# Seven half-depth products in place of eight for three pairs of feed-forward blocks

## The chip, the cores and the metric

The kernel runs on one core of a Trainium2 chip. The metric is the device time in microseconds (us) of one execution. Five engines of the core work here: TensorE (PE, matrix products), VectorE (DVE), ScalarE (ACT), GpSimd (POOL) and SyncE (SP), whose queue issues most of the DMAs. Each engine works through its own list in order and waits on semaphores that the others raise.

## The reference

Two decoder layers work on 256 tokens of width 1024. Each has a mixer (two kinds of attention, not touched here) and a feed-forward part, to which the change belongs:

```
h = _rmsnorm(x, g_pre_ffn) * (1.0 + sc2) + sh2
f = (jax.nn.silu(h @ w_gate) * (h @ w_up)) @ w_down
return x + gt2 * _rmsnorm(f, g_post_ffn)
```

The hidden width is 2816. Everything is float32. The vectors sc2, sh2 and gt2 come from a product of silu(c) with `w_ada`, which the kernel accumulates in 512 KB pieces beside the other work.

## The kernel before

**Tiles.** The 256 tokens are two tiles of 128 (t = 0, 1). The activations lie transposed, in eight slices k of 128 rows of depth. A float32 product is made of three fast ones (`product`, L1481 to L1485): high part by high part, high by low of the weights, low by high. The hidden width is cut into 11 blocks j of 256 columns. A block is projected upwards by `up(l, j, t)`: 128 tokens by 512 columns (256 of the gate, 256 of the other branch) over eight slices, so 24 products of 128x512 for each t. Then ScalarE takes the silu, VectorE multiplies the halves (`ffn_m`, L1460, called a gate below), TensorE transposes the result (`turn_m`), ScalarE and VectorE split it into high and low parts, and `down_chunk(l, j, t)` projects it downwards with 12 products of 128x512.

**Weights.** All weights come in units of 128x2048 elements (1 MB). An upward projection of a block uses two units (slices 0 to 3, and 4 to 7), a downward one uses one. A unit is loaded into one of three `raw` buffers (SP, L468), ScalarE copies its high part to `w_hi` (L654) and VectorE subtracts for its low part `w_lo` (L1006). `w_hi` and `w_lo` are rings of five: the split of a unit waits until TensorE has used the unit five places earlier. The load of a unit waits for the split of the unit that lay in its buffer.

**Order.** All orders are written out by hand. For block j TensorE runs `up(j, 0)`, `up(j, 1)`, `down_chunk(j-1, 0)`, `turn_m(j, 0)`, `turn_m(j, 1)`, `down_chunk(j-1, 1)`. VectorE runs the split of one unit, the two gates, a split, a piece of the modulation vector (L1034), the two low parts of `ffn_m` (L1208) and a split. In layer 1 eight such pieces lie in blocks 0 to 7, one a block. After the eighth, GpSimd sums the vector over the partitions (PARTITION_ALL_REDUCE, L555).

## Time and profile before

| what | us |
|---|---|
| median of 3 runs | 846.04 |
| lowest and highest run | 845.91, 846.12 |
| the profiled execution | 845.91 |
| its span, first to last instruction | 844.1 |

The span is what the views below cover. The rest of an execution's time lies around it. TensorE is busy for 99% of the span, VectorE for 77%, ScalarE for 53%. Layer 1's feed-forward part runs from about 651 us to 838 us of the span. What is busy on TensorE is modelled: a product of 128x512 has a duration of 0.39 us in the rows, while the next one starts 0.23 us after it. In a row of a timeline the first number is the start, the second the duration, and in brackets stands how long the engine was idle before it and what ended that.

### The profile page before, as it was taken

The numbers are of one execution on the slowest core, as the hardware profiler recorded it, in microseconds if no ns is written. First come the engines' busy times: TensorE is split into PE (matmuls) and PEld (weight loads), VectorE is DVE, ScalarE is ACT, GpSimd is POOL, SyncE is SP. The second block draws the span as 40 slices with busy tenths as digits, with TensorE's granted clock in tenths as the row PEclk, the third lists the DMA queues.
The fourth block names the chain that finished last, engine by engine and source line by source line (L and its number), as shares of the span: only waits on it lengthen the run. The fifth ranks groups of instructions, "written<-read, shape, count | busy, mean of one in ns | idle before, by whom it ended". The sixth has DMA issues, their size and how long they took to land.

```text
span 844.1 us, 11561 instructions
## 1 busy us (share of the span) xinstructions
PE 835.2 (99%) x4155; PEld 694.2 (82%) x4155; DVE 646.4 (77%) x1150; ACT 446.3 (53%) x723; POOL 122.2 (14%) x92
## 2 busy tenths in 40 slices
PE   8999999999999999999999999999999999999997
PEld 6877888888888888888888788888888888888885
DVE  5798889888788776786689899898787866545743
ACT  5665555565757434433476556565565745334422
POOL 5500300301210021030420040040040000000300
PEclk9999999999999999999999999999999999999999
DMA  8996676576417788787438756766642576664611
GB/s 342 415 360 233 217 257 252 203 270 224 144 57 299 290 282 324 251 305 278 183 120 310 284 204 219 276 214 243 221 150 100 198 276 213 247 236 177 223 51 51
DMA packets 34795, 194.10 MB, mean 230 GB/s; under 512 B 4273, under 2 KB 4529, under 8 KB 17714
## 3 DMA queue, kind: packets, MB, share of 16 engines
q1 hardware_dynamic: 33410, 189.64, 61.4%
q0 software_dynamic: 1328, 3.71, 1.3%
q8 instruction: 34, 0.56, 0.3%
q14 instruction: 23, 0.19, 0.1%
HBM read 192.29 MB, written 1.05 MB: 229 GB/s over the span
## 4 chain that ended last, share of the span: by engine, by line
PE 95%; DMA 3%; DVE 1%; SPq 0%; issue 0%; DVEq 0%; ACT 0%
PE ps L1483 26%; PE ps L1485 26%; PE ps L1484 26%; PE ps L1596 4%; DMA wide_t<-scale_first 3%; PE ps L1660 2%; PE ps L1520 1%; PE ps L1521 1%; PE ps L1527 1%; PE ps L1681 1%; PE ps L1682 1%; PE ps L1659 1%; PE ps L1680 1%; PE ps L1642 1%; PE ps L1612 1%; PE ps L1834 0%
## 5 line engine op out<-in xcount | busy, mean ns | idle before, releaser
L1006 DVE TENSOR_TENSOR w_lo<-raw,w_hi 128x2048 fp32r<-128x2048 f32 (+2 forms) x128 | 294.8, 2309 | 60.2 <-ACT w_hi L654 59.1
L1483 PE MATMUL ps<-w_hi,t_hi 128*128 128x512 f32 (+2 forms) x776 | 306.9, 395 | 1.0 <-DVE w_lo L1006 0.9
L1485 PE MATMUL ps<-w_hi,t_lo 128*128 128x512 f32 (+2 forms) x776 | 300.0, 387 | 0.0
L1484 PE MATMUL ps<-w_lo,t_hi 128*128 128x512 f32 (+2 forms) x776 | 299.4, 386 | 0.0
L654 ACT ACTIVATE w_hi<-raw 128x2048 fp32r<-128x2048 f32 (+2 forms) x130 | 244.8, 1885 | 25.5 <-DMA raw<-w_stream 16.9
L1483 PEld LDWEIGHTS ps<-w_hi,t_hi 128*128 128x128 f32 x776 | 145.8, 188 | 32.1 <-DVE w_lo L1006 1.9
L1485 PEld LDWEIGHTS ps<-w_hi,t_lo 128*128 128x128 f32 x776 | 145.7, 188 | 30.2
L1484 PEld LDWEIGHTS ps<-w_lo,t_hi 128*128 128x128 f32 x776 | 146.0, 188 | 27.6
L555 POOL PARTITION_ALL_REDUCE wide_t<-wide_t x20 | 80.0, 3998 | 555.7 <-DVE wide_t L1034 554.8
L1034 DVE SCALAR_TENSOR_TENSOR wide_t<-ada,cs,wide_t 128x1024 f32<-128x1024 f32 x80 | 110.3, 1379 | 1.0 <-DMA ada<-w_ada 0.7
L966 ACT ACTIVATE relu<-ps 128x256 f32<-128x256 f32 x44 | 17.0, 386 | 147.4 <-PE ps L1485 147.4
L1483 PE MATMUL ps<-w_hi,m_hi 128*128 128x512 f32 x208 | 84.3, 405 | 0.0
L1485 PE MATMUL ps<-w_hi,m_lo 128*128 128x512 f32 x208 | 81.4, 391 | 0.0
L1484 PE MATMUL ps<-w_lo,m_hi 128*128 128x512 f32 x208 | 81.0, 389 | 0.0
L1460 DVE TENSOR_TENSOR ffn_m<-relu,ps 128x256 f32<-128x256 f32 x44 | 18.2, 418 | 75.0 <-ACT relu L966 74.9
L727 ACT ACTIVATE qkT<-ps 128x512 f32<-128x512 f32 x24 | 14.4, 599 | 71.9 <-PE ps L1596 45.4
L1485 PEld LDWEIGHTS ps<-w_hi,m_lo 128*128 128x128 f32 x208 | 39.0, 188 | 8.6
L1484 PEld LDWEIGHTS ps<-w_lo,m_hi 128*128 128x128 f32 x208 | 39.2, 188 | 7.3
L1483 PEld LDWEIGHTS ps<-w_hi,m_hi 128*128 128x128 f32 x208 | 39.1, 188 | 7.1
L681 ACT ACTIVATE pj<-ps 128x384 f32<-128x384 f32 x32 | 15.7, 492 | 38.5 <-PE ps L1485 38.5
L747 ACT ACTIVATE m_hi<-ps 128x256 fp32r<-128x256 f32 (+1 forms) x48 | 17.3, 400 | 18.2 <-PE ps L1596 18.2
L545 POOL MEMSET wide_t<- 128x1024 f32 x10 | 9.6, 961 | 90.8 <-DVE x L1319 74.4
(226 smaller groups left out, 911.4 us busy)
## 6 DMA issues: line engine op xcount, KB each, us to landing
raw<-w_stream SPq DMA_DIRECT2D x126, 1024.0 KB, 5.2
ada<-w_ada SPq DMA_DIRECT2D x80, 512.0 KB, 5.6
wide_t<-gains POOLq DMA_DIRECT2D x7, 512.0 KB, 4.6
raw<-w_stream SPq DMA_DIRECT2D x4, 656.0 KB, 7.4
mixed<-scale_first SPq DMA_DIRECT2D x2, 1024.0 KB, 9.7
wide_t<-shift_first SPq DMA_DIRECT2D x4, 512.0 KB, 10.5
wide_t<-scale_first SPq DMA_DIRECT2D x2, 1024.0 KB, 12.7
ada<-shift_first SPq DMA_DIRECT2D x4, 512.0 KB, 12.5
```

Of the source, the lines that this page charges most:

```text
L555: nc.gpsimd.partition_all_reduce(acc[:, cols], tables[i][:, cols], P, bass.bass_isa.ReduceOp.add).then_inc(s_reduced, 1)
L654: nc.scalar.activation(w_hi[:, U % RING, a:n], src[:, a:n], ACT.Copy).then_inc(s_hi, 1)
L747: nc.scalar.activation(dst, src, ACT.Copy).then_inc(s_act_hi, 1)
L966: nc.scalar.activation(ffn_s[:, t, :], ps[:, QKT + t, 0:256], ACT.Silu).then_inc(s_silu, 1)
L1006: nc.vector.tensor_tensor(w_lo[:, U % RING, a:n], src[:, a:n], w_hi[:, U % RING, a:n].bitcast(F32), ALU.subtract).then_inc(s_lo, 1)
L1034: nc.vector.scalar_tensor_tensor(out=buf[:, :], in0=src, scalar=cs[:, k:k + 1], in1=buf[:, :], op0=ALU.mult, op1=ALU.add).then_inc(s_adaus ...
L1460: nc.vector.tensor_tensor(ffn_m[:, t, :], ffn_s[:, t, :], ps[:, QKT + t, 256:512], ALU.mult).then_inc(s_m, 1)
L1483: nc.tensor.matmul(dst, hi, w_h, start=first, stop=False)
L1484: nc.tensor.matmul(dst, hi, w_l, start=False, stop=False)
L1485: return nc.tensor.matmul(dst, lo, w_h, start=False, stop=last)
L1596: ins = nc.tensor.transpose(dst[:, i * P:(i + 1) * P], blk, ident)
L1660: nc.tensor.matmul(ps[:, SCO, P:3 * P], q[:, P:SEQ], k, start=True, stop=True).then_inc(s_sco, 1)
```

## The change

In layer 1, blocks (3, 4), (6, 7) and (8, 9) are projected upwards in pairs (`TWINS`). The two token tiles, the two halves of the depth and the two blocks make a product of two-by-two matrices of tiles. Such a product is made with seven tile products in place of eight, at the price of sums of tiles before it and after it. Each tile product is 12 products of 128x512 (`seventh`, over four slices). Layer 0 is as before.

- **Sums of the tokens** are made once (`add_tokens`, at block 1): five VectorE instructions, one over 128x2048 elements, four over 128x512. ScalarE splits off the high part of the result, and at block 2 VectorE the low part (`sums_low`).
- **Sums of the weights** (`add_weights`): the seven products use seven weight units in place of four. Four of the seven are sums, which VectorE makes with four additions over 128x2048 for each pair, in the memory of `mixed` and of `raw`. All seven are split into high and low parts.
- **Sums of the products** (`add_products`): five VectorE additions over 128x512 for each pair, and one copy by ScalarE. Product 5 continues in the accumulator of product 1, and product 6 in that of product 4, once those have been read: TensorE waits for the second and the third of the additions there.
- **Loads**: each weight is still loaded once. One unit of each pair goes to `mixed`. The other three stay in the three `raw` buffers until products 4 and 5 have been split.
- **The pieces** of the modulation vector move: blocks 0, 1, 2 and 5 of layer 1 take 1, 2, 2 and 3 of them.

```diff
+TWINS = ((), (3, 6, 8))
+TWIN_SUMS = (1, 4, 3, 6)
...
-    return (1, 1, 1, 1, 1, 1, 1, 1, 0, 0, 0), (9,)
+    return (1, 2, 2, 0, 0, 3, 0, 0, 0, 0, 0), (8,)
...
+            def twin_hi(l, j):
+                p = twin_no(l, j)
+                ahead, behind = up_splits(l, j)
+                split_hi(l, ahead[0])
+                wait_twin(act, l, j, 0)
+                nc.scalar.activation(twin_a, ps[:, QKT, :], ACT.Copy).then_inc(s_kept, 1)
+                for u in behind[:4]:
+                    split_hi(l, u)
+                act.wait_ge(s_twin, 5 * p + 4)
+                silu(l, j, 0, twin_c[:, 0:256], -1.0)
+                silu(l, j, 1, twin_b[:, 0:256], -1.0)
+                split_hi(l, behind[4])
+                silu(l, j + 1, 0, ps[:, QKT, 0:256])
+                act.wait_ge(s_twin, 5 * p + 5)
+                silu(l, j + 1, 1, twin_a[:, 0:256])
+                split_hi(l, behind[5])
+                m_hi_split(l, j, 0)
+                m_hi_split(l, j, 1)
+                split_hi(l, behind[6])
+                split_hi(l, behind[7])
+                m_hi_split(l, j + 1, 0)
+                m_hi_split(l, j + 1, 1)
...
+            def add_weights(U, e):
+                start = U - e
+                upper, lower, corner = (stored(*SOURCE[start + i]) for i in (4, 5, 2))
+                dve.wait_ge(s_lo, U + 1)
+                if e == 0:
+                    dve.wait_ge(upper[1], upper[2])
+                    nc.vector.tensor_tensor(w_sum, w_sum, upper[0], ALU.add).then_inc(s_w_sum, 1)
+                    dve.wait_ge(lower[1], lower[2])
+                    nc.vector.tensor_tensor(upper[0], upper[0], lower[0], ALU.add).then_inc(s_w_sum, 1)
+                else:
+                    nc.vector.tensor_tensor(w_sum, w_sum, (lower if e == 1 else corner)[0], ALU.add).then_inc(s_w_sum, 1)
...
+            def twin_lo(l, j):
+                ahead, behind = up_splits(l, j)
+                up = slice(256, 512)
+                split_lo(l, ahead[0])
+                split_lo(l, behind[0])
+                split_lo(l, behind[1])
+                add_products(l, j, twin_a, twin_a, SCO, 3, 1)
+                add_products(l, j, twin_b, twin_a, PTB, 1, 2)
+                split_lo(l, behind[2])
+                add_products(l, j, twin_b, twin_b, OUT, 4, 3)
+                split_lo(l, behind[3])
+                add_products(l, j, twin_c, twin_a, PTB, 5, 4)
+                gate_m(l, j, 0, twin_c[:, up], -1.0)
+                gate_m(l, j, 1, twin_b[:, up], -1.0)
+                add_products(l, j, twin_a, twin_a, OUT, 6, 5)
+                split_lo(l, behind[4])
+                m_lo_split(l, j, 0)
+                m_lo_split(l, j, 1)
+                gate_m(l, j + 1, 0, ps[:, QKT, up])
+                gate_m(l, j + 1, 1, twin_a[:, up])
+                split_lo(l, behind[5])
+                if j in ffn_pieces(l)[1]:
+                    make_table(4 * l + 3 + ffn_pieces(l)[1].index(j))
+                split_lo(l, behind[6])
+                split_lo(l, behind[7])
+                m_lo_split(l, j + 1, 0)
+                m_lo_split(l, j + 1, 1)
...
+                    if j == sums_step(l):
+                        add_tokens(l)
+                    elif j == sums_step(l) + 1:
+                        sums_low(l)
...
+            def twin_up(l, j):
+                p = twin_no(l, j)
+                before = 2 * (l * N_FF + j - 1)
...
+                pe.wait_ge(s_m, before + 1)
+                seventh(0, QKT, t_hi, t_lo, 0, 0)
+                pe.wait_ge(s_sums_lo, sums_no(l))
+                pe.wait_ge(s_act_lo, l * N_SPLIT + turn_no("m", 2 * (j - 1)))
+                seventh(1, PTB, sums_hi, sums_lo, 1, 1)
+                pe.wait_ge(s_kept, p + 1)
+                seventh(2, QKT, t_hi, t_lo, 1, 0, first=False)
+                pe.wait_ge(s_m, before + 2)
+                seventh(3, SCO, sums_hi, sums_lo, 0, 0)
+                pe.wait_ge(s_act_lo, l * N_SPLIT + turn_no("m", 2 * (j - 1) + 1))
+                seventh(4, OUT, sums_hi, sums_lo, 0, 1)
+                pe.wait_ge(s_twin, 5 * p + 2)
+                seventh(5, PTB, sums_hi, sums_lo, 1, 0, first=False)
+                pe.wait_ge(s_twin, 5 * p + 3)
+                seventh(6, OUT, t_hi, t_lo, 1, 1, first=False)
+                down_chunk(l, j - 1, 0)
+                turn_m(l, j, 0)
+                pe.wait_ge(s_twin, 5 * p + 5)
+                turn_m(l, j, 1)
+                down_chunk(l, j - 1, 1)
+                down_chunk(l, j, 0)
+                turn_m(l, j + 1, 0)
+                turn_m(l, j + 1, 1)
+                down_chunk(l, j, 1)
```

Two places of VectorE's list show how the work moves. The first is layer 1's blocks 0 to 2, in the kernel before. Here `w_lo<-raw,w_hi` is the split of a weight unit, `ffn_m<-relu,ps` a gate, `m_lo<-ps,m_hi` the low part of a gated block, and `wide_t<-ada,cs,wide_t` a piece.

```order
L1006 TENSOR_TENSOR w_lo<-raw,w_hi 128x2048
L1208 TENSOR_TENSOR m_lo<-ps,m_hi 128x2x128
L1460 TENSOR_TENSOR ffn_m<-relu,ps 128x256 x2
L1006 TENSOR_TENSOR w_lo<-raw,w_hi 128x2048
L1034 SCALAR_TENSOR_TENSOR wide_t<-ada,cs,wide_t 128x1024
L1208 TENSOR_TENSOR m_lo<-ps,m_hi 128x2x128 x2
L1006 TENSOR_TENSOR w_lo<-raw,w_hi 128x2048 x2
L1460 TENSOR_TENSOR ffn_m<-relu,ps 128x256 x2
```

The same place in the changed kernel, from the same split to the gates of block 1:

```order
L1156 TENSOR_TENSOR w_lo<-raw,w_hi 128x2048
L1179 TENSOR_TENSOR token_sums<-t_hi,t_lo 128x2048
L1180 TENSOR_TENSOR token_sums<-token_sums 128x4x128
L1181 TENSOR_TENSOR token_sums<-token_sums 128x4x128
L1182 SCALAR_TENSOR_TENSOR token_sums<-token_sums 128x4x128
L1184 SCALAR_TENSOR_TENSOR token_sums<-token_sums 128x4x128
L1442 TENSOR_TENSOR m_lo<-ps,m_hi 128x2x128
L1212 TENSOR_TENSOR ffn_m<-relu,ps 128x256 x2
```

And on from there, to the gates of block 2:

```order
L1156 TENSOR_TENSOR w_lo<-raw,w_hi 128x2048
L1268 SCALAR_TENSOR_TENSOR wide_t<-ada,cs,wide_t 128x1024
L1442 TENSOR_TENSOR m_lo<-ps,m_hi 128x2x128 x2
L1156 TENSOR_TENSOR w_lo<-mixed,w_hi 128x2048
L1168 TENSOR_TENSOR mixed<-mixed,raw 128x2048
L1170 TENSOR_TENSOR raw<-raw 128x2048
L1268 SCALAR_TENSOR_TENSOR wide_t<-ada,cs,wide_t 128x1024
L1190 TENSOR_TENSOR token_sums_lo<-token_sums,token_sums_hi 128x2048
L1156 TENSOR_TENSOR w_lo<-mixed,w_hi 128x2048
L1172 TENSOR_TENSOR mixed<-mixed,raw 128x2048
L1212 TENSOR_TENSOR ffn_m<-relu,ps 128x256 x2
```

Five token sums now stand ahead of the gates of block 1. Between those gates and the gates of block 2 stand three additions of weights, one more piece, and the low part of the token sums.

The second place is where pair (6, 7) meets pair (8, 9), from the last sum of products of the first to the low parts of block 7. Before, the two blocks' share here was the repeating pattern of a gate pair, three splits, a piece and two low parts.

```order
L1156 TENSOR_TENSOR w_lo<-mixed,w_hi 128x2048
L1168 TENSOR_TENSOR mixed<-mixed,raw 128x2048
L1170 TENSOR_TENSOR raw<-raw 128x2048
L1442 TENSOR_TENSOR m_lo<-ps,m_hi 128x2x128 x2
L1212 TENSOR_TENSOR ffn_m<-relu,ps 128x256
L1212 TENSOR_TENSOR ffn_m<-relu,pj 128x256
L1156 TENSOR_TENSOR w_lo<-mixed,w_hi 128x2048
L1172 TENSOR_TENSOR mixed<-mixed,raw 128x2048
L1156 TENSOR_TENSOR w_lo<-raw,w_hi 128x2048
L1156 TENSOR_TENSOR w_lo<-mixed,w_hi 128x2048
L1172 TENSOR_TENSOR mixed<-mixed,raw 128x2048
L1442 TENSOR_TENSOR m_lo<-ps,m_hi 128x2x128 x2
```

Two additions stand ahead of block 6's low parts, and two more among the splits ahead of block 7's.

## Rows read from the trace of the kernel before

**Rows 1.** The page: busy time, and TensorE and its granted clock in 40 slices.
```profile
PE 835.2 (99%) x4155; PEld 694.2 (82%) x4155; DVE 646.4 (77%) x1150; ACT 446.3 (53%) x723; POOL 122.2 (14%) x92
...
PE   8999999999999999999999999999999999999997
...
PEclk9999999999999999999999999999999999999999
```

**Rows 2.** A stretch: length, busy PE, PEld, DVE, ACT, POOL, granted clock, DMA share, GB/s.
```profile
655.00:831.00 176.00, 176.00 (x801) 145.16 (x801) 104.38 (x96) 77.82 (x85) 9.09 (x5) 1.00 0.53 194
```

**Rows 3.** Timeline of TensorE: start, duration, line, operation.
```profile
678.35 0.60 PE L1596 MATMUL ps<-const,ffn_m 128*128 128x128 f32 x4
...
698.34 0.39 PE L1483 MATMUL ps<-w_hi,t_hi 128*128 128x512 f32 x1
...
709.22 0.39 PE L1483 MATMUL ps<-w_hi,m_hi 128*128 128x512 f32 x1
```

**Rows 4.** Groups by line and shape: busy us, mean ns, idle before and releaser.
```profile
L1006 DVE TENSOR_TENSOR w_lo<-raw,w_hi 128x2048 fp32r<-128x2048 f32 x31 | 74.0, 2407 | 16.5 <-ACT w_hi L654 16.5
...
L1034 DVE SCALAR_TENSOR_TENSOR wide_t<-ada,cs,wide_t 128x1024 f32<-128x1024 f32 x8 | 10.2, 1280 | 0.0
...
L1460 DVE TENSOR_TENSOR ffn_m<-relu,ps 128x256 f32<-128x256 f32 x22 | 9.1, 419 | 51.7 <-ACT relu L966 51.7
...
L1242 DVE SCALAR_TENSOR_TENSOR pj<-pj,rstd,wide_t 128x512 f32<-128x512 f32 x4 | 2.8, 750 | 0.1
...
L1273 DVE TENSOR_TENSOR pj<-ps,wide_t 128x512 f32<-128x512 f32 x4 | 2.7, 680 | 0.0
...
L1280 DVE TENSOR_TENSOR pj<-x,wide_t 128x448 f32<-128x448 f32 x2 | 1.2, 615 | 0.0
...
L1280 DVE TENSOR_TENSOR pj<-x,wide_t 128x96 f32<-128x96 f32 x4 | 1.0, 245 | 0.0
```

**Rows 5.** Timeline of VectorE in blocks 0, 1, 2, 3 and 4.
```profile
674.25 2.29 DVE L1006 TENSOR_TENSOR w_lo<-raw,w_hi 128x2048 fp32r<-128x2048 f32 x1 [0.56 <-ACT w_hi L654]
676.46 0.42 DVE L1208 TENSOR_TENSOR m_lo<-ps,m_hi 128x256 fp32r<-128x256 f32 x1
676.79 0.74 DVE L1460 TENSOR_TENSOR ffn_m<-relu,ps 128x256 f32<-128x256 f32 x2
...
694.83 2.29 DVE L1006 TENSOR_TENSOR w_lo<-raw,w_hi 128x2048 fp32r<-128x2048 f32 x1 [1.38 <-ACT w_hi L654]
...
704.40 0.42 DVE L1460 TENSOR_TENSOR ffn_m<-relu,ps 128x256 f32<-128x256 f32 x1 [1.01 <-ACT relu L966]
...
721.19 0.42 DVE L1460 TENSOR_TENSOR ffn_m<-relu,ps 128x256 f32<-128x256 f32 x1 [0.99 <-ACT relu L966]
```

**Rows 6.** Timeline of ScalarE: splits of high parts in blocks 0, 1 and 3.
```profile
662.77 3.71 ACT L654 ACTIVATE w_hi<-raw 128x2048 fp32r<-128x2048 f32 x2
...
672.28 1.93 ACT L654 ACTIVATE w_hi<-raw 128x2048 fp32r<-128x2048 f32 x1 [2.12 <-DMA raw<-w_stream]
...
698.60 1.92 ACT L654 ACTIVATE w_hi<-raw 128x2048 fp32r<-128x2048 f32 x1 [0.53 <-PE ps L1485]
```

**Rows 7.** Timeline of GpSimd and VectorE around the eighth piece's sum.
```profile
782.43 7.48 POOL L555 PARTITION_ALL_REDUCE wide_t<-wide_t  x2 [125.99 <-DVE wide_t L1034]
782.91 8.15 DVE L1006 TENSOR_TENSOR w_lo<-raw,w_hi 128x2048 fp32r<-128x2048 f32 x2
```

**Rows 8.** The tile raw: landing of its loads, then one issue on SyncE's timeline.
```profile
DMA to landing us min/median/max: 4.6/5.5/7.3
...
697.15 0.33 SPq L468 DMA_DIRECT2D raw<-w_stream  x1
```

**Rows 9.** The end: the last matmul, then half-microsecond stretches (granted clock third from the end).
```profile
837.99 0.39 PE L1485 MATMUL ps<-w_hi,m_lo 128*128 128x512 f32 x1
...
842.00:842.50 0.50, 0.00 (x0) 0.00 (x0) 0.00 (x0) 0.00 (x0) 0.00 (x0) 1.00 1.05 410
842.50:843.00 0.50, 0.00 (x0) 0.00 (x0) 0.00 (x0) 0.00 (x0) 0.00 (x0) 0.64 0.98 377
```

More of the change, by code:

```diff
@@ L347, in hybrid_decoder_trunk, with stored @@
         shift_at = (wide_t[:, 0, :], wide_t[:, 1, :], ada[:, 0, :], ada[:, 1, :])
[L349 to L363 removed]
+        def stored(kind, n):
+            if kind == "spare":
+                return scale_at[n], s_spare[n], 16
+            if kind == "sum":
+                return w_sum, s_sum_in, 16 * (n + 1)
+            return raw[:, n % RAW, :], s_raw[n % RAW], 16 * (n // RAW + 1)
+        def raw_at(U):
+            return stored(*SOURCE[U])
         cs_wide = qkT[:, 0:KT * 32].rearrange("p (k n) -> p k n", k=KT)
@@ L949, in _ @@
                 border(l, True)
-                for j in range(N_FF):
-                    ahead, behind = up_splits(j)
+                for j, *both in ffn_steps(l):
+                    if both:
+                        twin_hi(l, j)
+                        continue
+                    ahead, behind = up_splits(l, j)
                     for u in ahead[:1]:
@@ new lines, in add_tokens @@
+            def add_tokens(l):
+                upper, lower = slice(0, 4), slice(4, KT)
+                one, two = slice(0, P), slice(P, 2 * P)
+                dve.wait_ge(s_act_lo, l * N_SPLIT + turn_no("h2", 3))
+                link(nc.vector.tensor_tensor(sums[:, :, :], t_hi[:, :, :].bitcast(F32), t_lo[:, :, :].bitcast(F32), ALU.add))
+                link(nc.vector.tensor_tensor(sums[:, lower, two], sums[:, lower, two], sums[:, upper, two], ALU.subtract))
+                link(nc.vector.tensor_tensor(sums[:, upper, two], sums[:, upper, one], sums[:, upper, two], ALU.subtract))
+                link(nc.vector.scalar_tensor_tensor(out=sums[:, upper, one], in0=sums[:, lower, two], scalar=-1.0,
+                                                    in1=sums[:, upper, one], op0=ALU.mult, op1=ALU.subtract))
+                nc.vector.scalar_tensor_tensor(out=sums[:, lower, one], in0=sums[:, lower, one], scalar=-1.0,
+                                               in1=sums[:, upper, one], op0=ALU.mult, op1=ALU.subtract).then_inc(s_sums, 1)
@@ new lines, in sums_low, with add_products @@
+            def sums_low(l):
+                dve.wait_ge(s_sums_hi, sums_no(l))
+                nc.vector.tensor_tensor(sums_lo[:, :, :], sums[:, :, :], sums_hi[:, :, :].bitcast(F32),
+                                        ALU.subtract).then_inc(s_sums_lo, 1)
+            def add_products(l, j, to, of, bank, after, count):
+                p = twin_no(l, j)
+                wait_twin(dve, l, j, after)
+                if count == 1:
+                    dve.wait_ge(s_kept, p + 1)
+                else:
+                    dve.wait_ge(s_twin, 5 * p + count - 1)
+                nc.vector.tensor_tensor(to, of, ps[:, bank, :], ALU.add).then_inc(s_twin, 1)
@@ L1441, in _ @@
                 border(l, True)
-                for j in range(N_FF):
-                    ahead, behind = up_splits(j)
+                for j, *both in ffn_steps(l):
+                    if both:
+                        twin_lo(l, j)
+                        continue
+                    ahead, behind = up_splits(l, j)
                     many = ffn_pieces(l)[0][j]
+                    if j == sums_step(l):
+                        add_tokens(l)
+                    elif j == sums_step(l) + 1:
+                        sums_low(l)
                     for u in ahead[:1]:
@@ L1887, in up, with seventh @@
                 ins.then_inc(s_up, 1)
+            def twin_up(l, j):
+                p = twin_no(l, j)
+                before = 2 * (l * N_FF + j - 1)
+                def seventh(e, bank, hi, lo, half, t, first=True):
+                    U = BASE[l] + twin_unit(l, j) + e
+                    pe.wait_ge(s_lo, U + 1)
+                    for i in range(4):
+                        k, tokens, cols = 4 * half + i, slice(t * P, (t + 1) * P), slice(512 * i, 512 * i + 512)
+                        parts = ((hi, w_hi), (hi, w_lo), (lo, w_hi))
+                        for n, (h, w) in enumerate(parts):
+                            ins = nc.tensor.matmul(ps[:, bank, :], h[:, k, tokens], w[:, U % RING, cols],
+                                                   start=first and i + n == 0, stop=i + n == 5,
+                                                   skip_group_check=not first)
+                    ins.then_inc(s_used, 1)
+                pe.wait_ge(s_m, before + 1)
[22 more added lines that the diff above has]
+                down_chunk(l, j, 1)
             def turn_m(l, j, t):
@@ L1966, in _ @@
                 turn_m(l, 0, 0)
-                for j in range(1, N_FF):
+                for j, *both in ffn_steps(l)[1:]:
+                    if both:
+                        twin_up(l, j)
+                        continue
                     up(l, j, 0)
```

205 lines of the change are left out of this document (145 added, 60 removed).

## The prediction

> **What bounds the kernel now.** I read the page first, then the stretches of layer 1's feed-forward part, then the groups by shape and the timelines of the engines. The page shows TensorE busy for 99% and in every slice of 40, at the full granted clock [rows 1]. From 655 to 831 us it is busy for all 176 us, while VectorE has 104.4 us of work and ScalarE 77.8 [rows 2]. So TensorE's list is the time here, and a product less is time less, as long as the others keep up. The reader should also see how little slack VectorE has in the end: it waits 51.7 us for silus in front of its gates and 16.5 us in front of its splits [rows 4], and the change fills that.
>
> TensorE's pace: `up(3, 0)` and `up(3, 1)`, 48 products, take from 698.34 to 709.22 us [rows 3], so 0.2267 us each. A block lasts 721.19 - 704.40 = 16.79 us [rows 5]: 72 products are 16.32, and the two transposes of a block 0.47.
>
> **What is removed.** Each pair loses one tile product of 12 products: 3 x 12 x 0.2267 = 8.2 us of TensorE. A pair falls from 33.6 to 30.9 us.
>
> **What VectorE gets.** A split takes 2.21 us from start to next start (674.25 to 676.46) and is known to the others 2.32 us after its start (694.83, issue at 697.15) [rows 5, 8]. Gates and low parts follow at 0.33 (0.42 for one, 0.74 for two) [rows 5]. A piece is 1.28 long, 1.20 to the next [rows 4].
>
> The additions of weights are not in the trace. The nearest rows are float32 sums with two SBUF inputs: 245 ns for 96 elements and 615 for 448 [rows 4], so 1.051 ns an element, and for 2048 elements 245 + 1952 x 1.051 = 2297 ns: the length of a split. I take the split's 2.21 from start to start, 2.30 as the upper bound, and 1.1 (twice the rate) as the lower, since no row has this shape in plain float32. The Trainium skill ("VectorE: DVE Perf Modes", section "Why `tensor_tensor` can't do 2×_2P or 4×") says that float32 instructions with one tensor input can run at twice the rate, and those with two cannot. By that rule the additions cost what the splits cost, and the bound of 1.1 falls away. The rows above bear it out for the small sums only.
>
> A sum of products reads PSUM and SBUF at 128x512: 0.68 long, 0.61 to the next [rows 4]. The token sums: 2.29, then two at 0.69 and two at 0.75 [rows 4], each waiting for the one before, for which I add 0.07 four times: 5.45. Their low part is a split, 2.21.
>
> New work in all: three more units a pair, 9 x 2.21 = 19.9; 12 additions, 26.5; 15 sums of products, 9.2; token sums 7.7. That is 63.2 us on top of 104.4, so 167.6 us. TensorE would need 176 - 8.2 = 167.8. VectorE has no slack left, and it works in order among handoffs, so TensorE will wait. For a pair followed by a pair VectorE has nine splits, four additions, five sums, four gates and four low parts: 19.9 + 8.8 + 3.1 + 2.6 = 34.4 us against 30.9.
>
> **Where TensorE waits.** I follow both lists from the same point, 676.46 us, with ScalarE's splits at 1.80 apart (3.71 for two less 1.91) and ready about 1.95 after their start (672.28, and VectorE at 674.25), and TensorE's results known 0.26 after a unit (698.34 to 698.60) [rows 3, 5, 6].
>
> *Block 1.* The token sums stand ahead of the gates: 676.46 + 5.45 + 0.33 (low part of block 0) + 0.33 (gate) + 0.11 = 682.68. The transposes of block 1 stand at 678.35 [rows 3]. Wait: 4.3.
>
> *Block 2.* ScalarE makes the high part of the token sums from 682.0 to 683.8 and only then splits a weight unit, which VectorE has at 685.77. Then it runs seven of the size of a split (three splits, three additions, the low part of the token sums) 15.5, two pieces 2.4, two low parts 0.7, a gate 0.3, and two waits on itself 0.2: 704.85, known at 704.96. TensorE leaves its last wait at 682.68, with 0.57 for the transposes (0.1 of it a second wait) and 72 products, 16.32, ahead of it: 699.57. Wait: 5.4.
>
> *Pair (3, 4).* Product 5 needs the second sum of products. From block 2's first gate VectorE has 0.3, a split 2.2, a piece 1.2, two low parts 0.7, a split 2.2, an addition 2.3, a piece 1.2, three splits 6.6 and two sums 1.3, a handoff 0.1: 723.05. TensorE again has 0.57 and 72 products: 721.85. Wait: 1.2. The next unit's load waits until the sum in `raw` is split, at 717.3; with a landing in 4.7 us, near the least of 4.6 [rows 8], ScalarE starts at 722.0, and product 6 waits 1.1. With the median of 5.5 this becomes 1.9.
>
> *Pair (6, 7).* The eighth piece now ends in block 5, so GpSimd's sum falls on the pair. Beside it two splits took 8.15 us [rows 7] in place of 2.21 + 2.29: some 3.6 more, before in a place with slack. From product 6 of pair (3, 4), at 726.88, TensorE runs 108 products and four transposes to the end of `up(5, 1)`, 752.30; a handoff, a silu (0.28) and a high part later VectorE can split, at 754.79: five splits 11.1, two pieces 2.4, two low parts 0.7, an addition 2.3, the delay 3.6, two sums 1.3, a handoff 0.1: 776.27. TensorE has 84 more products and two transposes after 752.30 (19.04 + 0.47): 771.82. Wait: 4.5.
>
> *From pair to pair.* Product 5's unit is split at 772.7; only then is the next unit loaded (4.7), made high (1.95) and low (2.21); then come a sum 0.7, two silus 0.6 and the high part of the next pair's first unit: 784.82. Block 6's low parts stand behind ScalarE's split of product 1 of the next pair, which needs VectorE's addition: 784.82 + 2.2 + 0.1 + 2.2 + 0.1 (VectorE), + 1.8 + 0.4 (ScalarE), + 0.4 = 792.13, against 787.72. Wait: 4.4. Product 1 of pair (8, 9) needs the accumulator that block 7's low part frees, and that stands behind three splits and two additions: 793.01 + 5 x 2.21 + 0.2 + 0.4 = 804.72, against 800.76. Wait: 4.0. After that VectorE has only splits, and nothing waits.
>
> Small waits beside these come to 0.3. Sum: 4.3 + 5.4 + 1.2 + 1.1 + 4.5 + 4.4 + 4.0 + 0.3 = 25.2 us of waits, less 8.2 of products: 17.0 longer. The same lists, followed for the kernel before, end TensorE at 838.1; the trace has 837.99 + 0.39 [rows 9]. The tail behind it stays. The profiled execution's 845.91 becomes 862.9; it lies 0.1 below the median, so 863.
>
> **Bounds.** With landings at 5.5 the waits are 26.8 (+18.6, 864.5). With handoffs shorter by 0.06 each it is +15.8 (861.7). With additions at 2.30 it is at most 12 x 0.09 = 1.1 more (864). With additions at 1.1, 3.3 goes from block 2, 1.2 from pair (3, 4), 1.1 from each of the next two, 2.2 from the last: +8.1, 854.
>
> **Rivals.**
> *The clock falls in the waits.* After the last matmul's end at 838.38 the granted clock holds until about 842.6 and then halves [rows 9]: 4.2 us of idleness did it. Four of my waits are longer (4.3, 5.4, 4.5, 4.4), one is 4.0. Against it: these are at the edge. The return of the clock is not in the trace; with 5 us at half speed each fall costs 2.5. But the loss after the first wait is taken off the second, and that after the third off the fourth, since TensorE then comes later to the same release. About 2.8 us remain: 866. With 10 us each, 7.8 remain: 871. The Trainium skill ("TensorE: Matmul & The Clock Gate", section "HAM oscillation — how this bites in real kernels") warns of just this, gaps in front of products that throttle the clock; by it this rival would be the forecast.
>
> *The additions are cheaper than a split*: 854, as above, down to 850 if the token sums run at twice the rate too. For it: no row shows such an addition. Against: the slope of the small sums.
>
> *The five units of lead carry VectorE's surplus (the other side).* If the ring let VectorE fall behind without anyone waiting, only the totals would count, 167.6 against 167.8, and all 8.2 us would be gained: 837.8. This is decided at the transposes of block 1: if they start at 678.4 as before, it is so. Against it stands that gates and sums of products are in VectorE's list between the splits, and the ring does not run ahead of those.
>
> *The change does not do what it says* would need 36 fewer products not to be there; the instruction lists show them gone (3496 rows of TensorE's list before, 3460 after).
>
> **Chances.** Forecast 0.57 (861 to 865.5), the clock 0.27 (864.5 to 871), cheaper additions 0.11 (850 to 860), the other side 0.05. The range 856 to 870 holds the first, most of the second and part of the third. A difference below 0.2% (1.7 us) is about what a measurement here cannot tell from none. Faster 0.04, within it 0.01, slower 0.95.
>
> **What would show it.** In the new profile: TensorE idle in front of the transposes of blocks 1 and 2 for 4 and 5 us, released by VectorE's gates; in front of product 5 of pair (6, 7) and of `down_chunk(6, 0)`, 4 to 5 each; VectorE above 95% busy from 676 to 810; the weight additions at 2.29 us; two splits at about 4 us beside GpSimd's sum, at pair (6, 7). The prediction is wrong if TensorE's idle time in this part is below 20 us, if the additions are short, or if the clock is low for more than 5 us in all.

## The result and the profile after

The changed kernel takes 865.5 us (median of four runs, 864.72 to 865.99) against 845.97 (four runs, 845.4 to 846.12): a ratio of 1.0231, with a 95% interval of 1.0214 to 1.0249. That is 19.5 us more. The forecast was 863 (17.0 more), and the range 856 to 870. The profiled execution took 865.86 us, its span 864.0.

The page of the changed kernel, first busy time and then the 40 slices, answers to [rows 1]:

```profile
PE 836.0 (97%) x4119; PEld 692.2 (80%) x4119; DVE 709.3 (82%) x1192; ACT 464.5 (54%) x736; POOL 122.8 (14%) x92
...
PE   8999999999999999999999999999999889979897
...
PEclk9999999999999999999999999999999989998999
```

The matmuls are fewer by 36 and VectorE has 62.9 us more to do (63.2 were forecast). Four of TensorE's slices late in the span are 8 or 7 and two of the clock's are 8; before, all of these were 9. So the loss lies where the pairs are, from 676 us on. One stretch of the changed kernel, with the columns of [rows 2] and the same bounds:

```profile
655.00:831.00 176.00, 158.17 (x674) 127.68 (x673) 158.91 (x129) 91.39 (x89) 11.11 (x5) 0.94 0.51 192
```

TensorE is idle for 176 - 158.17 = 17.8 us, where it was never idle before, and the mean clock is 0.94. The next view says who ends these waits: per engine, line and releaser, the total in us, the number and the longest, from 670 us on.

```profile
PE ps L1832 <- DVE ffn_m L1212: 7.5, 2, 4.0
PE ps L2138 <- DVE pj L1201: 4.6, 1, 4.6
PE ps L2138 <- issue: 3.7, 1, 3.7
PE ps L1719 <- DVE m_lo L1442: 2.1, 1, 2.1
```

There are five, at the transposes of blocks 1 and 2 (L1832), product 5 of pair (6, 7), product 1 of pair (8, 9) (both L2138) and `down_chunk(6, 0)` (L1719). VectorE released four by name. The fifth is put down to "issue"; VectorE makes block 7's low parts right before it ends, as the rows of VectorE show below. In the kernel without the token sums (further down) the same wait carries VectorE's name, at L1439, its line of the low parts:

```profile
PE ps L2131 <- DVE m_lo L1439: 3.6, 1, 3.6
```

TensorE's timeline has the five in order (start, duration, line, operation, and in brackets the idle time before). Compare the second row with [rows 3], where the transposes of block 1 stand at 678.35.

```profile
678.21 0.39 PE L1721 MATMUL ps<-w_hi,m_lo 128*128 128x512 f32 x1
682.55 0.85 PE L1832 MATMUL ps<-const,ffn_m 128*128 128x128 f32 x4 [3.96 <-DVE ffn_m L1212]
...
704.80 1.12 PE L1832 MATMUL ps<-const,ffn_m 128*128 128x128 f32 x4 [3.53 <-DVE ffn_m L1212]
...
777.14 0.80 PE L2138 MATMUL ps<-w_hi,token_sums_hi 128*128 128x512 f32 x1 [4.58 <-DVE pj L1201]
...
793.17 0.50 PE L1719 MATMUL ps<-w_hi,m_hi 128*128 128x512 f32 x1 [2.08 <-DVE m_lo L1442]
...
805.80 0.59 PE L2138 MATMUL ps<-w_hi,token_sums_hi 128*128 128x512 f32 x1 [3.68 <-issue]
...
857.91 0.39 PE L1721 MATMUL ps<-w_hi,m_lo 128*128 128x512 f32 x1
```

The last row answers to [rows 9]: the last matmul stands at 857.91 in place of 837.99, so 19.9 us are there by then, and the tail is as before.

VectorE's timeline shows what stood ahead of the releases. First the token sums and the gates of block 1, then one addition of weights and the stretch ahead of product 5 of pair (6, 7), and last the low parts of block 7:

```profile
676.65 2.29 DVE L1179 TENSOR_TENSOR token_sums<-t_hi,t_lo 128x2048 f32<-128x2048 f32 x1
...
682.09 0.74 DVE L1212 TENSOR_TENSOR ffn_m<-relu,ps 128x256 f32<-128x256 f32 x2
...
761.51 2.29 DVE L1172 TENSOR_TENSOR mixed<-mixed,raw 128x2048 f32<-128x2048 f32 x1
763.72 1.28 DVE L1268 SCALAR_TENSOR_TENSOR wide_t<-ada,cs,wide_t 128x1024 f32<-128x1024 f32 x1
764.92 6.53 DVE L1156 TENSOR_TENSOR w_lo<-raw,w_hi 128x2048 fp32r<-128x2048 f32 x2
771.37 4.32 DVE L1156 TENSOR_TENSOR w_lo<-mixed,w_hi 128x2048 fp32r<-128x2048 f32 x1
775.62 1.47 DVE L1201 TENSOR_TENSOR pj<-pj,ps 128x512 f32<-128x512 f32 x2
...
805.28 0.75 DVE L1442 TENSOR_TENSOR m_lo<-ps,m_hi 128x256 fp32r<-128x256 f32 x2
805.95 4.48 DVE L1156 TENSOR_TENSOR w_lo<-raw,w_hi 128x2048 fp32r<-128x2048 f32 x2
```

The addition takes 2.29 us, the size of a split. GpSimd's sum runs from 765.10 to 774.55, and beside it two splits take 6.53 and the next one 4.32, where two alone take 4.48 (805.95) and one 2.29. [Rows 7] showed the same in a harmless place.

The granted clock, in stretches of 2 us (columns as in [rows 2]), around blocks 1 and 2 and products 5 and 1:

```profile
680.00:682.00 2.00, 0.00 (x0) 0.00 (x0) 1.93 (x4) 0.13 (x1) 0.00 (x0) 1.00 1.01 426
682.00:684.00 2.00, 1.45 (x6) 1.18 (x7) 0.83 (x3) 2.00 (x2) 0.00 (x0) 0.78 0.98 406
684.00:686.00 2.00, 2.00 (x6) 1.55 (x5) 0.38 (x1) 2.00 (x3) 0.00 (x0) 0.50 0.11 45
686.00:688.00 2.00, 2.00 (x9) 1.59 (x9) 2.00 (x2) 1.94 (x2) 0.00 (x0) 0.87 0.02 4
...
708.00:710.00 2.00, 2.00 (x7) 1.52 (x6) 2.00 (x4) 0.20 (x1) 0.00 (x0) 0.50 0.03 8
...
774.00:776.00 2.00, 0.00 (x0) 0.00 (x0) 2.00 (x2) 0.00 (x0) 1.10 (x2) 0.82 0.79 332
776.00:778.00 2.00, 0.85 (x2) 0.77 (x3) 1.90 (x3) 1.77 (x1) 0.00 (x0) 0.50 0.92 203
...
806.00:808.00 2.00, 2.00 (x6) 1.50 (x6) 2.00 (x2) 0.00 (x0) 0.00 (x0) 0.50 0.04 8
808.00:810.00 2.00, 2.00 (x8) 1.59 (x7) 2.00 (x2) 0.00 (x0) 0.00 (x0) 0.65 0.46 70
```

The clock drops to half, the 1.2 GHz level, after four of the five waits (3.96, 3.53, 4.58 and 3.68 us), and not after the one of 2.08. It comes back some 3.5 to 6 us after TensorE is at work again. Not every fall lies in the wait: at block 1 it comes at about 683.1 and at product 1 at 806.0, when TensorE is already back (682.55 and 805.80). Read the matmul counts: 6 records in 2 us at half clock, 10 or 11 at full.

### The profile page after: what moved, and what is told of

It is laid out like the page before. It is cut to its first block, busy times and chain, and to the rows that moved or that the text cites. A ratio compares the mean times of both kernels' runs of the same rounds, so it can differ in the third digit from the quotient of the medians.

```text
span 864.0 us, 11580 instructions
## 1 busy us (share of the span) xinstructions
PE 836.0 (97%) x4119; PEld 692.2 (80%) x4119; DVE 709.3 (82%) x1192; ACT 464.5 (54%) x736; POOL 122.8 (14%) x92
## 4 chain that ended last, share of the span: by engine, by line
PE 86%; DVE 5%; DMA 4%; issue 3%; ACT 1%; SPq 0%; DVEq 0%; ACTq 0%
PE ps L1719 22%; PE ps L1721 21%; PE ps L1720 21%; PE ps L2138 6%; PE ps L1832 4%; DMA wide_t<-scale_first 3%; DVE w_lo L1156 2%; PE ps L1896 2%; ACT w_hi L769 1%; PE ps L1756 1%; PE ps L1757 1%; PE ps L1763 1%; PE ps L1917 1%; PE ps L1918 1%; PE ps L1895 1%
## 5 line engine op out<-in xcount | busy, mean ns | idle before, releaser
L1156 DVE TENSOR_TENSOR w_lo<-raw,w_hi 128x2048 fp32r<-128x2048 f32 (+2 forms) x125 | 286.2, 2295 | 52.0 <-ACT w_hi L769 50.8
L1719 PE MATMUL ps<-w_hi,t_hi 128*128 128x512 f32 (+2 forms) x680 | 269.6, 396 | 2.0 <-DVE t_lo L1320 1.1
L1721 PE MATMUL ps<-w_hi,t_lo 128*128 128x512 f32 (+2 forms) x680 | 262.7, 386 | 0.0
L1720 PE MATMUL ps<-w_lo,t_hi 128*128 128x512 f32 (+2 forms) x680 | 262.1, 385 | 0.0
L769 ACT ACTIVATE w_hi<-raw 128x2048 fp32r<-128x2048 f32 (+2 forms) x127 | 238.8, 1883 | 39.8 <-DMA raw<-w_stream 26.4
L1719 PEld LDWEIGHTS ps<-w_hi,t_hi 128*128 128x128 f32 x680 | 127.8, 188 | 29.5 <-DVE w_lo L1156 3.2
L1721 PEld LDWEIGHTS ps<-w_hi,t_lo 128*128 128x128 f32 x680 | 127.7, 188 | 26.4
L1720 PEld LDWEIGHTS ps<-w_lo,t_hi 128*128 128x128 f32 x680 | 128.0, 188 | 23.9
L1719 PE MATMUL ps<-w_hi,m_hi 128*128 128x512 f32 x208 | 86.2, 414 | 2.1 <-DVE m_lo L1442 2.1
L1719 PEld LDWEIGHTS ps<-w_hi,m_hi 128*128 128x128 f32 x208 | 40.1, 193 | 9.9 <-DVE m_lo L1442 2.5
L769 ACT ACTIVATE w_hi<-mixed 128x2048 fp32r<-128x2048 f32 x13 | 24.9, 1917 | 27.3 <-DVE mixed L1168 16.3
L1156 DVE TENSOR_TENSOR w_lo<-mixed,w_hi 128x2048 fp32r<-128x2048 f32 x13 | 31.7, 2439 | 2.0 <-ACT w_hi L769 2.0
```

What stands on the lines that cost most here:

```text
L769: nc.scalar.activation(w_hi[:, U % RING, a:n], src[:, a:n], ACT.Copy).then_inc(s_hi, 1)
L1156: nc.vector.tensor_tensor(w_lo[:, U % RING, a:n], src[:, a:n], w_hi[:, U % RING, a:n].bitcast(F32), ALU.subtract).then_inc(s_lo, 1)
L1719: nc.tensor.matmul(dst, hi, w_h, start=first, stop=False)
L1720: nc.tensor.matmul(dst, hi, w_l, start=False, stop=False)
L1721: return nc.tensor.matmul(dst, lo, w_h, start=False, stop=last)
```

## The experiments

The theory: VectorE has no slack, and TensorE waits at the places of the forecast's list; the clock then falls in the waits, and only what no later wait gives back is lost. The rivals: the additions alone, the token sums alone, GpSimd's sum, or two pairs back to back are the whole cost. The kernel before took 845.8 to 845.9 us (medians) beside all of these.

### Keep TensorE busy in the waits

```diff
+IDLE_FILL = {1: 14, 2: 18}
...
+                if l and t == 0 and j in IDLE_FILL:
+                    fill(PTB, t_hi[:, 0, 0:P], t_hi[:, 0:2, :], 2 * SEQ, IDLE_FILL[j])
                 pe.wait_ge(s_m, 2 * (l * N_FF + j) + t + 1)
...
+                if j == 8:
+                    fill(SCO, t_hi[:, 0, 0:P], t_hi[:, 0:2, :], 2 * SEQ, 12)
                 pe.wait_ge(s_sums_lo, sums_no(l))
```

The wait for the earlier low parts (`s_act_lo`) moves ahead of the filling. The results of the added products are not used.

> The changed kernel with idle-time products added: 14 and 18 products of 128x512 (0.2267 us each, results unused) in front of the transposes of blocks 1 and 2, 12 in front of product 1 of pair (8, 9). They are shorter than the waits there (4.0, about 5, 4.0 us), so no list gets longer if VectorE sets the end of each wait. Theory (the granted clock falls in long waits and that costs 2 to 3 us of the 19.5): three of the four falls go, the one at product 5 of pair (6, 7) stays and is given back at the next wait: 862.5 to 863.5 us. Rival (the falls cost nothing, since TensorE waits for VectorE anyway): unchanged, 865.5.

Measured: 863.82 us (863.45 to 864.22), ratio 1.0214 (1.0198 to 1.0229), so 1.7 less than the changed kernel. Three of the four falls are gone (the clock is 1.00 in 682 to 688, 704 to 710 and 806 to 810), and the one at product 5, which had no filling, is still there:

```profile
684.00:686.00 2.00, 2.00 (x10) 1.65 (x9) 0.80 (x1) 2.00 (x4) 0.00 (x0) 1.00 0.05 18
...
778.00:780.00 2.00, 2.00 (x6) 1.52 (x6) 2.00 (x3) 0.00 (x0) 0.00 (x0) 0.50 1.02 418
...
806.00:808.00 2.00, 2.00 (x10) 1.64 (x9) 2.00 (x2) 0.00 (x0) 0.00 (x0) 1.00 0.00 0
```

Three falls cost about 6.1 us of pace (working below) and taking them away gave 1.7. That is what the last of them costs, 2 x 0.50 + 2 x 0.35 = 1.7, the only one of the three with no wait of TensorE's behind it. The other two had been paid out of later waits. The timeline bears this out: against the changed kernel the filled one is 0.4 us ahead at block 1's transposes (682.13), 0.8 at product 5 of pair (6, 7) (776.32) and 0.8 still at product 1 of pair (8, 9) (805.01), and 2.4 at the end of the span. With the first two falls gone, TensorE waits 0.76 us before product 5 and 0.76 before product 6 of pair (3, 4), where it had no wait before. The clock is a real cost, and a small one. The run ended a little above the expected range.

### Additions of weights over 16 columns

```diff
-                    nc.vector.tensor_tensor(w_sum, w_sum, upper[0], ALU.add)
+                    nc.vector.tensor_tensor(w_sum[:, 0:16], w_sum[:, 0:16], upper[0][:, 0:16], ALU.add)
```

and the two others in the same way. What it leaves out: the sums of weights, but for 16 of 2048 columns.

> The 12 additions of weights run over 16 columns in place of 2048, with all their waits (so the pair blocks' results are not the reference's). Theory (VectorE's list is late by the length of these additions): the waits at block 2, at products 5 and 6 of pair (3, 4) and at product 1 of pair (8, 9) go, 4.0 at block 1, 2.3 at product 5 of pair (6, 7) and 2.3 at the downward projection of block 6 stay: 846.0 + 0.6, plus up to 3 for a fall of the clock: 846 to 850 us. Rival (the handshake between TensorE and the sums of products makes the waits, whatever VectorE's load): they stay, above 860.

Measured: 848.89 (848.72 to 849.65), ratio 1.0039 (1.0024 to 1.0054): 16.6 less than the changed kernel. TensorE's waits in it:

```profile
PE ps L1832 <- DVE ffn_m L1212: 3.6, 1, 3.6
PE ps L2138 <- DVE pj L1201: 2.5, 1, 2.5
```

The wait at block 1 stays, as it is made by the token sums; block 2's and both from pair to pair go. The additions are 12 x 2.21 = 26.5 us of VectorE, and leaving them out is worth 16.6, the falls of the clock that go with them included. Two falls are left, after the wait of 3.6 and, unlike in the changed kernel, after one as short as 2.5 (low from about 769.7 to 773.1 us). The time lies in the expected range, and the rival (above 860) is out.

### Without the token sums, and without both

The token sums, their high and their low part are left out, and products 1, 3, 4 and 5 of each pair (`seventh(...)`) take `t_hi` and `t_lo`; the second run also makes the additions of weights over 16 columns.

> The token sums, their high and low part are left out, the products use the plain tokens (so the pair blocks' results are not the reference's). Theory: the waits of 4.0 us at block 1 and 5.4 at block 2 both go, since behind the token sums everything up to block 2's gates is late: 846.0 + 7.2 + 0 to 3 for the clock, 853 to 856.5 us. Rival (only the wait at block 1 is theirs, the one at block 2 is the weight additions'): 4 us less than 865.5, about 861.5.

> Both left out: the token sums, and the weight additions over 16 columns in place of 2048 (so the pair blocks' results are not the reference's). All 63 products' units, the splits, the sums of products and every wait between them stay. Theory (load in VectorE's list makes the waits, and GpSimd's sum beside the splits): only the waits at product 5 of pair (6, 7), 2.3, and at the downward projection of block 6, 2.3, are left, 8.2 of products gained: 846.0 - 3.5 = 842.5 us. Rival (the handshakes with the accumulators cost by themselves, 2 to 5 us a pair): 846 or more.

Measured: 855.5 (854.21 to 855.8), ratio 1.011 (1.0093 to 1.0127), without the token sums; 842.67 (842.42 to 843.64), ratio 0.9965 (0.9951 to 0.9979), without both. A train of 7.7 us on VectorE is worth 10 us: it stands in front of gates, at blocks 1 and 2. Without it the waits of 3.96 and 3.53 us there and the two falls behind them are gone; in their place TensorE waits 0.98 and 0.78 before products 5 and 6 of pair (3, 4). From pair (6, 7) on the waits are those of the changed kernel: 4.74, 2.08 and 3.60. The two causes do not add up: 16.6 and 10.0 alone, 22.8 together. With both gone the kernel is faster than before by 3.2 us, where 8.2 us of products are gone. So the rest of the change (splits, sums of products, GpSimd's sum) keeps 5 us. Waits of 2.66 at product 5 of pair (6, 7) and 1.61 at `down_chunk(6, 0)` are 4.3 of it; no fall follows them. Both expectations hit, and both rivals are out.

### One pair, with the token sums late

```diff
-TWINS = ((), (3, 6, 8))
+TWINS = ((), (7,))
-    return (1, 2, 2, 0, 0, 3, 0, 0, 0, 0, 0), (8,)
+    return (1, 1, 2, 2, 2, 0, 0, 0, 0, 0, 0), (9,)
...
                     add_pieces(many > 1)
+                    if j == 1 and TWINS[l]:
+                        add_tokens(l)
```

and ScalarE's high part of the token sums stands between the silus of block 2, their low part between its gates.

> One pair alone, (7, 8), the pieces in blocks 0 to 4 (1, 1, 2, 2, 2), the token sums at the end of block 1 behind its gates, their high part between block 2's silus and their low part between block 2's gates, where VectorE idled for 5 us. The result is the reference's. Theory (the waits come only from VectorE's work standing in front of gates and low parts): no wait is left, 12 products less: 846.0 - 2.7 = 843.3 us. Rival (a pair always costs its handshakes, 2.3 us at products 5 and 6 as in pair (3, 4)): 845.6 or more.

Measured: 843.3 (six runs, 842.82 to 843.43), ratio 0.997 (0.9958 to 0.9981). This is the fastest of those that leave nothing out, and beats both kernels: 2.5 us against 2.7 (12 x 0.2267) that a pair removes. Its page:

```profile
PE 831.9 (99%) x4143; PEld 691.2 (82%) x4143; DVE 668.4 (79%) x1168; ACT 452.9 (54%) x728; POOL 123.1 (15%) x92
...
PE   8999999999999999999999999999999999999997
```

No slice of TensorE but the first and the last is below 9, though VectorE has 22 us more than before. TensorE waits nowhere from 670 to 841 us. So a pair need not cost time by itself; what costs is VectorE's work where a gate or a low part stands behind it.

### The changed kernel with the token sums late

> The changed kernel's three pairs and pieces, but the token sums stand at the end of block 1 (behind its gates), their high part between block 2's silus and their low part between block 2's gates. The result is the reference's. Theory (between block 1's gates and pair (3, 4) VectorE is full, so a move there shifts the wait and does not remove it): the 4.0 at block 1 go, block 2 gets 5.1 and 2.3 in place of 5.4: 2.2 us less without the clock, and one long wait less gives the clock 0 to 1.5: 861.5 to 863.5. Rival (the place of the token sums is the fault, as in the single pair's kernel): both waits go, 9.4 less, 856.

Measured: 863.17 (862.68 to 863.33), ratio 1.0203 (1.0189 to 1.0217). The edit is the one of the run before, with the three pairs kept. It gives 2.3 us of the 10 that leaving the token sums out gave. TensorE's waits before the transposes of block 1 are gone, and those of block 2 are two:

```profile
700.24 0.69 PE L1832 MATMUL ps<-const,ffn_m 128*128 128x128 f32 x2 [4.89 <-DVE ffn_m L1212]
702.78 0.69 PE L1832 MATMUL ps<-const,ffn_m 128*128 128x128 f32 x2 [1.84 <-DVE ffn_m L1212]
```

Together 6.7 us, where blocks 1 and 2 had 7.5: VectorE has the same work to do before pair (3, 4). That is 0.8 of the 2.3; the rest is the clock, whose loss around blocks 1 and 2 is 2.7 us here and was 4.4. The theory holds, and its rival (856) is out.

### GpSimd's last sum made short

```diff
+                    if n == PARTS * DEPTH - 3:
+                        nc.gpsimd.tensor_copy(acc[:, 512 * half:512 * half + 16], tables[i][:, 512 * half:512 * half + 16]).then_inc(s_reduced, 1)
+                    else:
```

It leaves out the sum over partitions of the last scale vector.

> GpSimd's two sums over the partitions of the last modulation vector become copies of 16 columns (so the last norm's gain vector is not the reference's). Theory (3.6 us of delay of two splits beside it reach TensorE in full at product 5 of pair (6, 7)): that wait falls from 4.5 to about 1.0, product 6 then waits 1.1 for its load, and the fall of the clock there goes, which had been given back at block 6's wait: 2.5 to 3.5 us less than 865.5, 862 to 863 us. Rival (the delay is made good in the ring before product 5): 865.5.

Measured: 861.85 (four runs, 859.97 to 864.91), ratio 1.0192 (1.0174 to 1.021). The runs lie 5 us apart, wider than for any other kernel here. In the profiled one (864.91):

```profile
PE ps L1835 <- DVE ffn_m L1215: 7.4, 2, 3.9
PE ps L1722 <- DVE m_lo L1445: 4.8, 1, 4.8
...
PE ps L2141 <- DVE pj L1204: 1.6, 2, 1.1
```

The splits beside the copies take their usual 2.29 us again (4.49 for two). The wait for product 5 fell from 4.6 us to 0.5, and product 6 now waits 1.1, as was expected (both are in the `pj` row), but the one of `down_chunk(6, 0)` (`m_lo`) grew from 2.1 to 4.8. A wait taken away early comes back where VectorE's list is next late. The median lies just below the expected 862 to 863, while the profiled run, which was the slowest, gained only 1 us, so that the size of the gain is not settled. Why the runs differ so was not found.

### The first pair alone

```diff
-TWINS = ((), (3, 6, 8))
+TWINS = ((), (3,))
...
-    return (1, 2, 2, 0, 0, 3, 0, 0, 0, 0, 0), (8,)
+    return (1, 2, 2, 0, 0, 3, 0, 0, 0, 0, 0), (9,)
```

> Only pair (3,4) is left of the three; everything ahead of it (token sums in block 1, low part in block 2, pieces of the scale vector) stands as in the changed kernel. Theory (each wait is set by VectorE's list at its own place, so the first part costs the same alone): waits of 4.0 and 3.5 at the transposes of blocks 1 and 2 and about 2 at products 5 and 6, less 2.7 of products, plus what the clock's two falls leave, 1 to 2: 854.5 to 857.5. Rival (what costs is two pairs back to back, the first pair is nearly free): below 848.

Measured: 855.34 (854.88 to 856.4), ratio 1.0113 (1.0099 to 1.0127): 9.5 more than before. The first part waits as in the changed kernel, before the transposes of blocks 1 and 2:

```profile
682.21 1.07 PE L1832 MATMUL ps<-const,ffn_m 128*128 128x128 f32 x4 [3.83 <-DVE ffn_m L1212]
704.48 1.12 PE L1832 MATMUL ps<-const,ffn_m 128*128 128x128 f32 x4 [3.64 <-DVE ffn_m L1212]
```

The forecast's list gives 4.3 + 5.4 + 1.2 + 1.1 - 2.7 = 9.3 for this pair, without a word of the clock. Both falls are in the trace (a mean clock of 0.79 in 680 to 684, 0.50 in 704 to 708). They add little, because the waits behind them, at products 5 and 6, are gone in exchange. Two pairs back to back are not the whole cause: half of the 19.5 us is there without them. Beside the single pair (7, 8) above, this shows that the same 12 products less can be worth 2.5 us or cost 9.5, by where VectorE's new work stands. The two kernels differ in the place of the pair, of the token sums and of the pieces; what each of the three does by itself was not tried.

### Two pairs, in two arrangements

Pairs (5, 6) and (8, 9) with late token sums: pieces of the scale vector first as 1, 3, 3, 1 over blocks 0 to 3 (the first of the two added lines below), then as 1, 2, 2, 1 with the last two in block 7 (the second).

```diff
-TWINS = ((), (3, 6, 8))
+TWINS = ((), (5, 8))
-    return (1, 2, 2, 0, 0, 3, 0, 0, 0, 0, 0), (8,)
+    return (1, 3, 3, 1, 0, 0, 0, 0, 0, 0, 0), (8,)
+    return (1, 2, 2, 1, 0, 0, 0, 2, 0, 0, 0), (8,)
```

> Two pairs, (5, 6) and (8, 9), with a single block between them, pieces in blocks 0 to 3 (1, 3, 3, 1), token sums at the end of block 1, high part between block 2's silus, low part at the end of block 2. The result is the reference's. Theory: 24 products less, 5.4 us, and one wait of 2.0 us at block 4's transposes (GpSimd's sum and three weight additions ahead of its gates): 846.0 - 3.2 = 842.8 us, at most 0.5 better than one pair. Rival (with token sums late and pairs apart all waits go, the second pair brings its full 2.7): 840.6.

> Two pairs, (5,6) and (8,9), with the late token sums, as in the two-pair run before, but the eighth piece of the scale vector stands in block 7 in place of block 3, and no block has three pieces. Theory (in that run TensorE waited at blocks 2 and 4 because three pieces and GpSimd's sum stood in front of their gates): those waits go, GpSimd's sum falls beside pair (8,9), whose waits grow by up to 2: 841 to 844.5. Rival (two pairs cost VectorE too much wherever the sum stands): 846 or more.

Measured: the first 846.47 (11 runs, 843.8 to 848.46), ratio 1.0006 (0.9996 to 1.0015), 3.7 above what was expected; the second 847.72 (10 runs, 847.07 to 848.76), ratio 1.0021 (1.0012 to 1.0031), 3.2 above the end of its range. Both expectations missed. In the first, VectorE's timeline ahead of block 4's gates (a split, an addition, then the gates), TensorE's wait for them, and the stretch around it, with a mean clock of 0.89:

```profile
717.69 3.90 DVE L1156 TENSOR_TENSOR w_lo<-mixed,w_hi 128x2048 fp32r<-128x2048 f32 x1
721.63 4.21 DVE L1168 TENSOR_TENSOR mixed<-mixed,raw 128x2048 f32<-128x2048 f32 x1
...
732.49 0.74 DVE L1212 TENSOR_TENSOR ffn_m<-relu,ps 128x256 f32<-128x256 f32 x2
```

```profile
732.96 0.77 PE L1832 MATMUL ps<-const,ffn_m 128*128 128x128 f32 x4 [2.06 <-DVE ffn_m L1212]
```

```profile
728.00:736.00 8.00, 5.94 (x25) 4.47 (x24) 7.97 (x8) 4.76 (x6) 0.00 (x0) 0.89 0.01 2
```

GpSimd's sum fell on a split and an addition that stand before these gates, and cost 1.6 and 1.9 there; TensorE waited 2.06 us for the gates, and 1.35 for those of block 2, which stand behind the pieces. The expectation had the first of these waits, 2.0, and not the second. It had no fall of the clock either, and here one follows a wait of only 2.06: it starts at about 734.3, costs some 1.7 us, and no wait behind it gives it back. Together 845.8 - 5.4 + 2.06 + 1.35 + 1.7 = 845.5, where the median is 846.5. Of the 1.0 between, 0.7 is the count of idle time and the slower pace of some products, both explained below for the changed kernel (2 x 0.16 and 2 x 48 x 0.0043); the last 0.3 has no row. The second arrangement took GpSimd's sum away from there, and the theory's half on this was right: TensorE has no idle time from 672 to 792. But the sum then met the splits of pair (8, 9). VectorE in front of product 5, and TensorE's stretch:

```profile
786.22 6.53 DVE L1156 TENSOR_TENSOR w_lo<-raw,w_hi 128x2048 fp32r<-128x2048 f32 x2
792.67 4.32 DVE L1156 TENSOR_TENSOR w_lo<-mixed,w_hi 128x2048 fp32r<-128x2048 f32 x1
```

```profile
784.00:792.00 8.00, 8.00 (x36) 6.53 (x35) 8.00 (x4) 3.18 (x2) 5.51 (x2) 1.00 0.32 98
792.00:800.00 8.00, 3.42 (x13) 2.43 (x12) 7.90 (x5) 3.82 (x2) 4.40 (x2) 0.83 0.84 328
800.00:808.00 8.00, 8.00 (x28) 6.38 (x27) 5.98 (x8) 3.23 (x6) 0.00 (x0) 0.74 0.79 294
```

One wait of 8 - 3.42 = 4.6 us and the fall behind it, 2.8 (busy time x (1 - granted clock), in stretches of 2 us from 796 to 806), make 7.4, and 845.9 - 5.4 + 7.4 = 847.9, near the 847.7 measured. The expectation had let this wait grow by 2 and had left the clock out. The rival, that two pairs cost too much wherever the sum stands, is not refuted; both medians lie where it put them, at 846 or more. What the trace supports is that in the second arrangement the whole loss hangs on one place, and whether a place for the sum exists that costs nothing was not tried.

## Why the prediction came out as it did

The forecast was 863, and 865.5 was measured; the direction, the places and the releasers are as it said. Each step against the trace of the changed kernel (idle time before TensorE's instruction; the loss of a fall is an estimate, busy time x (1 - granted clock), summed over the 2 us stretches behind the wait):

| place | forecast wait | idle | loss of the fall behind it |
| --- | --- | --- | --- |
| block 1's transposes | 4.3 | 3.96 | 1.6 |
| block 2's transposes | 5.4 | 3.53 | 2.8 |
| pair (3, 4), products 5 and 6 | 2.3 | 0 | |
| pair (6, 7), product 5 | 4.5 | 4.58 | 2.5 |
| `down_chunk(6, 0)` | 4.4 | 2.08 | 0 |
| pair (8, 9), product 1 | 4.0 | 3.68 | 1.7 |
| small | 0.3 | | |
| sum | 25.2 | 17.8 | 8.6 |

**The releases were right, line by line.** VectorE's times set them, and idle time plus the loss just ahead of it comes to the forecast's wait: block 2 3.53 + 1.6 = 5.1 (5.4), `down_chunk(6, 0)` 2.08 + 2.5 = 4.6 (4.4). Products 5 and 6 of pair (3, 4) can't be read so, since the loss ahead of them, 2.8, is more than their wait; in the filled kernel, without that loss, they wait 0.76 each, 1.5 together (2.3). The first pair alone costs 9.5 where the list has 9.3, and one pair without waits was put at 843.3 and measured at 843.3.

**Additions and token sums**: right. An addition takes 2.29 us, the size taken from the slope of the small sums; the token sums take 5.1 from the first to the low part behind them (676.65 to 681.76), where 5.45 were taken. Leaving out the additions is worth 16.6 us, leaving out the token sums 10. The Trainium skill ("VectorE: DVE Perf Modes", section "Why `tensor_tensor` can't do 2×_2P or 4×") says that an instruction with two tensor inputs can't run in the doubled mode. This trace agrees, at 2.29 us for the addition as for the split.

**GpSimd's sum beside the splits**: right in place, a little small. It met three splits, not two, and cost (6.53 - 4.48) + (4.32 - 2.29) = 4.1 us, where 3.6 were taken.

**The clock: the term of the sum that was mis-sized.** "The clock falls in the waits" was a rival with 0.27, and the sum had 0 for it. The text held against it that the waits were at the edge of the 4.2 us that [rows 9] had shown at the end. The clock fell four times, also after 3.96, 3.68 and 3.53 us, and in other kernels here after 2.1 and 2.5. As that rival said, most of it is given back: 8.6 us of pace are lost, and 26.4 - 25.2 = 1.2 of it remains in the table's sum. The filled kernel puts the cost of three of the falls at 1.7. So what happened is the forecast's list of waits with this rival on top: 865.5 is the upper end of what the forecast allowed (861 to 865.5) and inside what the rival did. The rival's central value, 866, is nearer to the 865.5 than the forecast's 863.

**What the text said would make it wrong.** Two of its three conditions came true: TensorE's idle time in this part is 17.8 us, below 20, and the clock was low for about 20 us, more than 5. Both are one event, since time lost to the clock stands in the profile as busy. A condition on idle time alone was a bad test of a forecast of lost time; idle plus loss, 26.4, is the number to test. The third condition, short additions, did not come true. VectorE's share from 676 to 810 us is 125.67 of 134, 94%, where above 95 was forecast.

**The rest.** 17.8 + 8.6 - 8.2 = 18.2; the profiled run is 19.95 longer. Of the 1.7 between, 0.1 is there before block 1 (its last product ahead of the transposes starts at 678.21, before at 678.12), and 0.6 is a slower pace of some products (below). Another 0.8 comes from the way idle time is counted. It starts at the modelled end of a product, 0.39 after its start, while the next product would have started 0.23 after it: 678.21 + 0.39 + 3.96 comes to the 682.55 of block 1's transposes. So each of the five waits is 0.16 longer than its idle time. The last 0.2 has no row. The 8.6 is itself up to 0.5 too large, since at half clock products follow each other at 0.427 us and not at twice 0.2267; as much more would then be open.

**The other side** (the lead of five units carries VectorE's surplus) is out: the transposes of block 1 stand at 682.55. It comes true only in the kernel with one pair.

## What to carry to other kernels

Before trading TensorE's products for VectorE's sums, compare what the one loses with the slack of the other, and then place each new instruction by the gate or low part that is queued behind it: here 8.2 us of products cost 63 us of VectorE work, three such trades lose 19.5 us, and one, put where nothing waits, gains 2.5. A wait taken away comes back where the same engine is next late, so follow the list to its end before booking a gain. A fall of the clock behind a wait costs little if TensorE has to wait for another engine again later, and all of its loss if it is the last one.
